# Diagonal blocks packed by ScalarE for one transpose, and a new order of token rows and attention steps, in a fused DeltaNet and sliding-window layer

## The chip, the cores and the metric

The kernel runs on one core of one Trainium2 chip. The metric is the device time of one execution in microseconds (us), inputs in HBM and output back to HBM. Every number is float32.

## What is computed

One layer over 2048 tokens of width 1024. All eight input blocks of a token go through one RMS norm and one projection, whose columns feed two groups of heads:

```python
h = _rmsnorm(x, norm1_w)
gq, gk, gv, gz, gb, ga, aq, ak, av = split(h @ w_in)
# group A: 4 heads, gated delta rule in chunks
lower = strict(kb @ k.T * decay) + I
u, w = inverse(lower) @ (v * beta), inverse(lower) @ (kb * exp(gc))
v_new = u - w @ state
o = q_dec @ state + qk @ v_new
state = state * g_last + k_dec.T @ v_new          # one chunk after another
o_gdn = rms(o) * gdn_norm_w * silu(z)
# group B: 8 heads, window of 128 keys, softmax with a sink
o_attn = softmax(q @ k.T * d**-0.5 - slope * dist, sink) @ v
x = x + concat(o_gdn, o_attn) @ w_out
x = x + relu(rms(x) @ w1)**2 @ w2
```

The kernel takes chunks of 128 tokens ("tiles") for the delta rule, so a triangular 128x128 matrix is inverted for each of 4 heads and 4 tiles of a group.

## The kernel before

The sequence is cut into four groups of 512 tokens, and one loop over `g` runs all stages for a group. Each engine has its own program, written out by hand in order; engines meet only at semaphores, and an instruction that waits holds up all that stand behind it on its engine. Weights come in 96 units a group (a 1024x128 slab, 512 KB). A unit is loaded by SP, split by ScalarE into a high part (`split_hi`, w_h, L400) and by VectorE into a low part (`split_lo`, w_l, L720), and multiplied by TensorE in 24 matmuls (`unit`, all recorded at L1229, like most matmuls). `w_h` and `w_l` have two buffers each.

A group's stages, by their TensorE work:

1. Twelve convolution units, then units for the decay rows, attention v, k and four attention q units. In the loop over `j` of the q units each step also handles tile `t = j` of the delta rule: `decay`, `diagonal`, `products` (VectorE; `products` writes the strictly decayed Gram matrix `at_[:, t]`, signal `at_r`, L876), and `delta` (ScalarE, L506).
2. Four gate units `U_Z + m` (m = 0 to 3; called Z0 to Z3 below). In between come `token_rows(t)`: TensorE transposes v and k of a tile (L1336, L1341) into two PSUM banks, and VectorE scales them out (`value_rows`, signal `vb_r`, L1045; `key_rows`, signals `kb_r` and `kd_r`, L1054, L1056). A bank is used again only when the rows before are out.
3. The triangular inverse. VectorE inverts the 16x16 diagonal blocks: `gather` transposes them out of `at_` into block rows, `block_inverse` runs 19 small steps, `scatter` puts the result into the factors `ti` and `xi`. From there TensorE doubles the blocks over three levels (`masked`, `update`, `turn`).
4. Sixteen attention pairs n are spread over 19 steps `attend(k)` (k = 0 to 18) among levels, key states and tiles: step k starts pair k (`sc` on TensorE, then `scores` on VectorE and `exps` on ScalarE), finishes the softmax sum of pair k-1 on VectorE, whose division GpSimd does (L352), and transposes pair k-2 (`pt`) and multiplies pair k-3 with the values (`ov`) on TensorE.
5. The loop over the four tiles: `values`, `v_copy`, the sum for the next state, `new_state` (VectorE, L1088), the output matmuls, `out_square`, `out_mean`, `out_root` (ScalarE, L616, L618), `gated` (VectorE, L1100, L1105), `mix_hi`, `mix_lo`. `values(t)` waits for the state of tile t-1.
6. Eight output units (starting with `out_part` on the attention half), then the MLP in 64 units.

The orders of stages 2 and 5 in the kernel before, for TensorE:

```python
for m in range(GATE):
    unit(g, CONV, U_Z + m - CONV, A0 + (U_Z + m) % 2, hid)
    if 0 < m < GATE - 1:
        token_rows(m - 1)
...
for t in range(TILES):
    values(t)
    if t: out_mean(t - 1)
    attend(10 + 2 * t)
    if t == TILES - 1: attend(17)
    state_and_out(t)
    attend(11 + 2 * t if t < TILES - 1 else 18)
```

On VectorE, `gather`, `block_inverse` and `scatter` stand after `split_lo` of Z2 and before `split_lo` of Z3; the `vb_r` of tile 0 comes right after. GpSimd clears `ti` and `xi`, does the divisions of pairs 0 to 13, waits for `mlo` of tile 1, issues the load of `xs` and then does pairs 14 and 15.

Of the kernel before, what the change touches and what calls it, by code (L numbers as in the profile page):

```python
# [91 lines left out]
def build(nc, x, w, par, con, bias, out):  # L92
    with ExitStack() as ctx:
# [112 lines left out]
        MAX, NMAX, SUM, SEXP, RDEN = (slice(2 * i, 2 * i + 2) for i in range(5))  # L206

        def first_half(m, l):

            return m.rearrange("p (n two b) -> p n two b", two=2, b=BLOCK << l)[:, :, 0, :]  # L210
# [13 lines left out]
        def mix(t):  # L224

            return kb23[:, t] if t < 2 else qk[:, t - 2]

        def blocks(m, b):
# [4 lines left out]
        def flat(m):  # L233
            return m.rearrange("p h c -> p (h c)")

# [18 lines left out]
        tb_zeroed = ctx.enter_context(nc.semaphore("tb_zeroed"))  # L254
        blk_in = signal("blk_in", QUADS)
        blk_ext = signal("blk_ext", 4)
        blk_out = signal("blk_out", 2 * QUADS)
        blk = signal("blk", 19)
# [76 lines left out]
        def _(pool):  # L335
# [10 lines left out]
            with pool.Fori(0, GROUPS) as g:  # L346
# [16 lines left out]
                pool.nop(nofuse=True)  # L363
                nc.gpsimd.memset(ti[:], 0.0).then_inc(zeroed.sem, 1)
                nc.gpsimd.memset(xi[:], 0.0).then_inc(zeroed.sem, 1)  # L365
                for n in range(14):
                    probabilities(n)
# [3 lines left out]
                pool.dma_start(xs[:], x[g]).then_inc(x_loaded.sem, 16)  # L371
                for n in range(14, TILES * PAIRS):
                    probabilities(n)


# [16 lines left out]
        def _(act):  # L392
# [45 lines left out]
            with act.Fori(0, GROUPS) as g:  # L438
# [75 lines left out]


                act.wait_ge(unit_done.sem, unit_done.after(g, U_BA + 1))
                act.activation(rw[0:32, 0], ps[0:32, A0, :], ACT.Identity, scale=-1.0).then_inc(row_act.sem, 1)
# [24 lines left out]
                for j in range(PAIRS):  # L542
                    t = j
                    act.wait_ge(unit_done.sem, unit_done.after(g, U_AQ + j + 1))
                    act.copy(aq[:, j], ps[:, A0 + (U_AQ + j) % 2, :]).then_inc(copied.sem, 1)
                    split_hi(g, CONV, U_AQ + 2 + j - CONV)
                    norm_root(j)
                    decay(t)
                    key_log(t)
                    query_square(t)  # L550
                    delta(t)
                norm_root(PAIRS)

                act.wait_ge(B1["tok"].sem, B1["tok"].after(g, 1))
# [88 lines left out]
                attend(8)  # L643
                for t in range(TILES):
                    wt(B["p_wt"], t)
                    act.copy(ti[:, t], heads(lev(t))).then_inc(B["wtc"].sem, 1)
                attend(9)
                for t in range(TILES):
                    v_copy(t)
                    if t:  # L650
                        out_root(t - 1)
                    attend(10 + 2 * t)
                    if t == TILES - 1:
                        attend(17)
                    if t:
                        mix_hi(t - 1)
                    out_square(t)
                    attend(11 + 2 * t if t < TILES - 1 else 18)
                out_root(TILES - 1)
# [51 lines left out]
        def _(dve):  # L711
# [61 lines left out]
            with dve.Fori(0, GROUPS) as g:  # L773
# [131 lines left out]
                dve.tensor_scalar(sm[:, :, CB], sm[:, :, EGC], -1.0, None, ALU.mult).then_inc(B1["c1"].sem, 1)  # L905
                split_lo(g, CONV, U_Z + 2 - CONV)

# [10 lines left out]

                def quad(m, r):

                    return m[r][:, :, :, r].rearrange("j t h (b i) -> j i b (t h)", b=2)

                def by_block(m):

                    return m.rearrange("p (i b x) -> p i b x", b=2, x=BLOCK)
# [13 lines left out]

                def scatter():  # L940

                    flip = d1[:, 0].rearrange("p h c -> p (h c)")
                    rows = tb[:, 0:BLOCK * BLOCK].rearrange("p (r c) -> p r c", c=BLOCK)
                    for b in range(2):
                        own_half = prm[:, C_BLK + b:C_BLK + b + 1]
                        dve.tensor_scalar(by_block(tmp[:])[:, :, b], rows.rearrange("p r c -> p c r"), own_half, None,
                                          ALU.mult).then_inc(blk_ext.sem, 1)
                        dve.tensor_scalar(by_block(flip)[:, :, b], rows, own_half, None, ALU.mult).then_inc(blk_ext.sem, 1)
                    own(blk_ext, g, 4)
                    dve.wait_ge(zeroed.sem, zeroed.after(g, 2))  # L950
                    for n in range(QUADS):
                        r = slice(32 * n, 32 * n + 32)
                        dve.transpose(quad(ti, r), by_block(tmp[r])).then_inc(blk_out.sem, 1)
                        dve.transpose(quad(xi, r), by_block(flip[r])).then_inc(blk_out.sem, 1)

                def block_inverse():
# [183 lines left out]
                attend(8)  # L1140
                attend(9)
                for t in range(TILES):
                    attend(10 + 2 * t)
                    if t == TILES - 1:
                        attend(17)
                    if t:
                        gated(t - 1)
                    new_state(t)
                    attend(11 + 2 * t if t < TILES - 1 else 18)
                    out_square(t)  # L1150
                    if t:
                        mix_lo(t - 1)
# [74 lines left out]
        def _(pe):  # L1227
# [29 lines left out]
            with pe.Fori(0, GROUPS) as g:  # L1257
# [198 lines left out]

                def state_and_out(t):

                    wt(B["vnc"], t)
                    four(heads(outb(t, 1)), lambda o, h: mm(o, part(1, t)[:, h], v_new(t)[:, h]), B["p_su"])  # L1460
                    wt(B["qd_r"], t)
# [41 lines left out]
                attend(8)  # L1503
                for t in range(TILES):
                    key_states(t)
                attend(9)
                for t in range(TILES):
                    values(t)
                    if t:
                        out_mean(t - 1)  # L1510
                    attend(10 + 2 * t)
                    if t == TILES - 1:
                        attend(17)
                    state_and_out(t)
                    attend(11 + 2 * t if t < TILES - 1 else 18)

# [193 lines left out]
```

## Time and profile before

| | |
|---|---|
| median of 3 runs | 2623.86 us (2623.4 to 2624.37) |
| profiled execution | 2619.94 us, of it a span of 2618.4 us from first to last instruction |
| mean granted TensorE clock | 0.984 |
| busy: PE, DVE, ACT, POOL | 95%, 56%, 37%, 5% |
| HBM traffic | 88 GB/s over the span |

In the rows below PE is the matmul side of TensorE, DVE is VectorE, ACT is ScalarE and POOL is GpSimd. A row of a timeline has its start in us from the start of the span, its duration in us, the engine, the line, the operation, what it writes and reads, and how many instructions it merges; in brackets stands how long the engine was idle before it and what ended that. All four groups look alike; where no group is named, the rows are those of the first, whose stages 2 to 5 lie between 157 and 285 us.

### The profile page before, as it was taken

To read this page: it belongs to the slowest core of one execution; us is meant where nothing else is said; L and a number is where in the kernel's file an instruction comes from. 1 tells how busy PE (TensorE), PEld (TensorE's weight loads), DVE (VectorE), ACT (ScalarE), POOL (GpSimd) and SP (SyncE) were. 2 spreads that over 40 slices of the span, in tenths; PEclk is the share of its full clock that TensorE was granted. 3 is DMA by queue.
4 is the path that set the end of the run, shared out by engine and by line. 5 is a ranking of instruction groups with operands and counts; after the bars stand their busy time and mean duration, and the time that the engine had idled before them with its cause. 6 is when DMAs were issued, how large, how long until landed. Compare 5 with 4: busy or idle time off the path is not lost.

```text
span 2618.4 us, 36125 instructions
## 1 busy us (share of the span) xinstructions
PE 2490.5 (95%) x12446; PEld 2046.3 (78%) x12446; DVE 1463.5 (56%) x2220; ACT 957.8 (37%) x1741; POOL 129.6 (5%) x149
## 2 busy tenths in 40 slices
PE   5979999999997999999999799999999979999998
PEld 4868788888876778888887677888888767788887
DVE  5676564364667646345466765634556675552554
ACT  4436432223353733222335363222234536321222
POOL 0012000000000200000000120000000011000000
PEclk9989999999998999999999899999999989999999
DMA  4210223224321022233332112232432211232242
GB/s 148 96 49 18 89 89 102 92 96 152 106 88 41 25 90 97 96 96 120 129 106 81 41 42 81 96 99 94 138 116 101 73 33 47 91 98 97 94 140 77
DMA packets 62019, 233.16 MB, mean 89 GB/s; under 512 B 7232, under 2 KB 7232, under 8 KB 61248
## 3 DMA queue, kind: packets, MB, share of 16 engines
q1 hardware_dynamic: 55728, 202.64, 23.5%
q0 software_dynamic: 6160, 28.84, 3.0%
q8 instruction: 74, 1.21, 0.2%
q14 instruction: 57, 0.47, 0.1%
HBM read 223.06 MB, written 8.39 MB: 88 GB/s over the span
## 4 chain that ended last, share of the span: by engine, by line
PE 80%; issue 11%; DVE 4%; ACT 2%; POOL 2%; DMA 0%; ACTq 0%; POOLq 0%; DVEq 0%; SPq 0%
PE ps L1229 79%; POOL pp L352 1%; PE ps L1376 1%; ACT w_h L400 1%; DVE acc L728 0%; DVE w_l L720 0%; DMA stage<-w 0%; POOL xi L365 0%; DVE row L839 0%; DVE h_l L1168 0%; DVE cy L786 0%; DVE ht L734 0%; DVE nq L798 0%; DVE h_l L1110 0%; DVE h_l L1030 0%
## 5 line engine op out<-in xcount | busy, mean ns | idle before, releaser
L1229 PE MATMUL ps<-h_h,w_h 128*128 128x512 f32 x2016 | 800.9, 397 | 25.1 <-DVE h_l L1168 8.9
L1229 PE MATMUL ps<-h_l,w_h 128*128 128x512 f32 x2016 | 789.6, 392 | 0.0
L1229 PE MATMUL ps<-h_h,w_l 128*128 128x512 f32 x2016 | 789.3, 391 | 0.0
L720 DVE TENSOR_TENSOR w_l<-stage,w_h 128x1024 fp32r<-128x1024 f32 (+1 forms) x385 | 467.9, 1215 | 315.1 <-ACT w_h L400 302.7
L400 ACT CAST w_h<-stage 128x1024 fp32r<-128x1024 f32 (+1 forms) x385 | 399.9, 1039 | 579.6 <-PE ps L1229 571.3
L1229 PEld LDWEIGHTS ps<-h_h,w_h 128*128 128x128 f32 x2016 | 381.6, 189 | 119.5 <-issue 23.1
L1229 PEld LDWEIGHTS ps<-h_h,w_l 128*128 128x128 f32 x2016 | 381.5, 189 | 80.6
L1229 PEld LDWEIGHTS ps<-h_l,w_h 128*128 128x128 f32 x2016 | 382.0, 190 | 79.6 <-issue 2.9
L1229 PE MATMUL ps<-ff_h,w_h 128*128 128x512 f32 x1024 | 400.0, 391 | 0.0
L1229 PE MATMUL ps<-ff_h,w_l 128*128 128x512 f32 x1024 | 398.4, 389 | 0.0
L1229 PE MATMUL ps<-ff_l,w_h 128*128 128x512 f32 x1024 | 398.4, 389 | 0.0
L684 ACT ACTIVATE ff_h<-fb 128x512 f32 (+1 forms) x128 | 81.1, 633 | 482.3 <-DVE fb L1182 482.3
L1229 PEld LDWEIGHTS ps<-ff_h,w_h 128*128 128x128 f32 x1024 | 192.2, 188 | 40.9 <-issue 1.0
L1229 PEld LDWEIGHTS ps<-ff_l,w_h 128*128 128x128 f32 x1024 | 192.2, 188 | 40.7 <-issue 1.0
L1229 PEld LDWEIGHTS ps<-ff_h,w_l 128*128 128x128 f32 x1024 | 192.2, 188 | 39.8
L1182 DVE SCALAR_TENSOR_TENSOR fb<-ps,rt 128x512 f32<-128x512 f32 x128 | 88.6, 692 | 232.4 <-PE ps L1229 220.7
L1201 DVE TENSOR_TENSOR xs<-ps,xs 128x512 f32 (+1 forms) x64 | 44.3, 693 | 187.8 <-PE ps L1229 187.8
L786 DVE SCALAR_TENSOR_TENSOR cy<-raw,prm,cy 128x512 f32<-128x512 f32 x144 | 108.0, 750 | 14.6 <-DVE cy L782 6.9
L1189 DVE TENSOR_TENSOR ff_l<-ff,ff_h 128x512 f32 (+1 forms) x128 | 88.7, 693 | 27.8 <-ACT ff_h L684 15.5
L1186 DVE TENSOR_TENSOR ff<-fb 128x512 f32<-128x512 f32 x128 | 88.6, 692 | 13.3 <-DVE fb L1182 8.5
L450 ACT COPY raw<-ps 128x512 f32<-128x512 f32 x48 | 28.2, 587 | 148.6 <-PE ps L1229 148.6
L352 POOL TENSOR_TENSOR pp<-pp,att 128x384 f32<-128x384 f32 x64 | 63.3, 992 | 333.5 <-DVE att L1024 333.5
(195 smaller groups left out, 2045.6 us busy)
## 6 DMA issues: line engine op xcount, KB each, us to landing
stage<-w SPq DMA_DIRECT2D x385, 512.0 KB, 3.3
x_next<-x POOLq DMA_DIRECT2D x20, 512.0 KB, 6.3
xs<-x POOLq DMA_DIRECT2D x4, 2048.0 KB, 8.0
out<-xs POOLq DMA_DIRECT2D x32, 256.0 KB, 2.3
bia<-bias POOLq DMA_DIRECT2D x1, 1536.0 KB, 7.1
cst<-con SPq DMA_DIRECT2D x1, 704.0 KB, 4.9
prm<-par SPq DMA_DIRECT2D x1, 39.5 KB, 1.8
```

The source lines that it names most:

```text
L352: nc.gpsimd.tensor_tensor(pp[:, n % 2, :, HD:], pp[:, n % 2, :, HD:], att[:, n % 2, RDEN].unsqueeze(2).to_broadcast([P, 2, KEYS]), ALU.mul ...
L400: act.copy(w_h[:, b, 0:k], stage[:, s, 0:k]).then_inc(w_hi.sem, 1)
L450: act.copy(raw[:, s % 2, 3:], ps[:, A0 + s % 2, :]).then_inc(raw_ready.sem, 1)
L684: act.activation(ff_h[:, i * 4 + s, :], fb[:, s % 2], ACT.Square).then_inc(fh_ready.sem, 1)
L720: dve.tensor_tensor(w_l[:, b, 0:k], stage[:, s, 0:k], w_h[:, b, 0:k].bitcast(F32), ALU.subtract).then_inc(w_lo.sem, 1)
L786: dve.scalar_tensor_tensor(out=cy[:, s % 2], in0=raw[:, s % 2, j:j + TOK], scalar=convw(prm, m, j), in1=cy[:, s % 2], op0=ALU.mult, op1=AL ...
L1182: dve.scalar_tensor_tensor(out=fb[:, s % 2], in0=ps[:, s % 2, :], scalar=0.0, in1=rt[:], op0=ALU.max, op1=ALU.mult).then_inc(fb_ready.sem, 1)
L1186: dve.tensor_tensor(ff[:, s % 2], fb[:, s % 2], fb[:, s % 2], ALU.mult).then_inc(fp_ready.sem, 1)
L1189: dve.tensor_tensor(ff_l[:, i * 4 + s, :], ff[:, s % 2], ff_h[:, i * 4 + s, :].bitcast(F32), ALU.subtract).then_inc(ff_ready.sem, 1)
L1201: dve.tensor_tensor(xs[:, m, :], ps[:, s // 2 % 2, :], xs[:, m, :], ALU.add).then_inc(res.sem, 1)
L1229: return pe.matmul(o, a, b, start=start, stop=stop)
L1376: last = pe.transpose(o[:, e, c], pp[:, n % 2, e, c * P:c * P + P], I)
```

## The change

It has three parts.

The first is the way of the diagonal blocks. Before, `gather` made four transposes of 32 partitions straight out of `at_`. Now ScalarE copies the blocks of each tile as soon as `at_` is written (`pack`, four copies of 32 partitions a tile, 16 in a group) side by side into the first quarter of `xi`, and `gather` is one transpose over 128 partitions. `xi` is cleared by GpSimd only after that. `scatter` keeps its eight transposes; its four scaling instructions are ordered by target, with a wait after the first two.

The second is the order around it. On VectorE `split_lo` of Z2 moves behind `gather`, and `split_lo` of Z3 from behind `scatter` to the middle of `block_inverse`. On TensorE the token rows of tiles 0 and 1 come one gate unit later: behind Z2 and Z3.

The third is the order of the last attention steps: each goes one place sooner from `attend(10)` on, and `state_and_out` is split, so that in the last tile `attend(18)` stands before the output matmuls. On ScalarE `out_root` and `mix_hi` of the tile before now stand behind the attention step. GpSimd issues the load of `xs` after all 16 pairs.

```diff
+        def quadrant(n):
+            return slice(32 * n, 32 * n + 32)
+        diag_in = flat(xi[:, 0])
...
         @block.gpsimd
                 nc.gpsimd.memset(ti[:], 0.0).then_inc(zeroed.sem, 1)
+                pool.wait_ge(blk_in.sem, blk_in.after(g, 1))
+                pool.nop(nofuse=True)
                 nc.gpsimd.memset(xi[:], 0.0).then_inc(zeroed.sem, 1)
-                for n in range(14):
+                for n in range(TILES * PAIRS):
                     probabilities(n)
 
                 pool.wait_ge(B["mlo"].sem, B["mlo"].after(g, 2))
                 pool.nop(nofuse=True)
                 pool.dma_start(xs[:], x[g]).then_inc(x_loaded.sem, 16)
-                for n in range(14, TILES * PAIRS):
-                    probabilities(n)
...
         @block.scalar
+                def pack(t):
+                    wt(B["at_r"], t)
+                    act.nop(nofuse=True)
+                    for n in range(QUADS):
+                        r = quadrant(n)
+                        act.copy(by_block(diag_in[r])[:, :, :, HEADS * t:HEADS * t + HEADS].rearrange("j i b h -> j h b i"),
+                                 at_[r, t][:, :, r].rearrange("j h (b i) -> j h b i", b=2)).then_inc(packed.sem, 1)
...
                     query_square(t)
                     delta(t)
+                    if t < TILES - 1:
+                        pack(t)
                 norm_root(PAIRS)
+                pack(TILES - 1)
...
+                w_copy(0)
+                w_copy(1)
                 attend(9)
+                w_copy(2)
+                w_copy(3)
+                attend(10)
                 for t in range(TILES):
                     v_copy(t)
+                    attend(11 + 2 * t)
                     if t:
                         out_root(t - 1)
-                    attend(10 + 2 * t)
+                        mix_hi(t - 1)
                     if t == TILES - 1:
-                        attend(17)
-                    if t:
-                        mix_hi(t - 1)
+                        attend(18)
                     out_square(t)
-                    attend(11 + 2 * t if t < TILES - 1 else 18)
+                    if t < TILES - 1:
+                        attend(12 + 2 * t)
...
         @block.vector
-                split_lo(g, CONV, U_Z + 2 - CONV)
...
                 def gather():
-                    own(B["at_r"], g, TILES)
-                    for n in range(QUADS):
-                        r = slice(32 * n, 32 * n + 32)
-                        dve.transpose(by_block(tmp[r]), quad(at_, r)).then_inc(blk_in.sem, 1)
-                    own(blk_in, g, QUADS)
+                    dve.wait_ge(packed.sem, packed.after(g, packed.per_group))
+                    dve.transpose(tmp[:], diag_in).then_inc(blk_in.sem, 1)
+                    own(blk_in, g, 1)
...
                     for b in (4, 8):
+                        if b == 8:
+                            split_lo(g, CONV, U_Z + 3 - CONV)
...
                 gather()
+                split_lo(g, CONV, U_Z + 2 - CONV)
                 block_inverse()
                 scatter()
-                split_lo(g, CONV, U_Z + 3 - CONV)
...
                 attend(8)
                 attend(9)
-                for t in range(TILES):
-                    attend(10 + 2 * t)
-                    if t == TILES - 1:
-                        attend(17)
+                attend(10)
+                for t in range(TILES):
+                    attend(11 + 2 * t)
                     if t:
                         gated(t - 1)
                     new_state(t)
-                    attend(11 + 2 * t if t < TILES - 1 else 18)
+                    attend(12 + 2 * t)
                     out_square(t)
...
         @block.tensor
                     unit(g, CONV, U_Z + m - CONV, A0 + (U_Z + m) % 2, hid)
-                    if 0 < m < GATE - 1:
-                        token_rows(m - 1)
+                    if m >= 2:
+                        token_rows(m - 2)
...
-                for t in range(TILES):
-                    key_states(t)
+                key_states(0)
+                key_states(1)
                 attend(9)
+                key_states(2)
+                key_states(3)
+                attend(10)
                 for t in range(TILES):
                     values(t)
                     if t:
                         out_mean(t - 1)
-                    attend(10 + 2 * t)
+                    attend(11 + 2 * t)
+                    state_sum(t)
                     if t == TILES - 1:
-                        attend(17)
-                    state_and_out(t)
-                    attend(11 + 2 * t if t < TILES - 1 else 18)
+                        attend(18)
+                    tile_out(t)
+                    if t < TILES - 1:
+                        attend(12 + 2 * t)
```

## Rows read from the trace of the kernel before

**Rows 1.** The page's chain that ended last, shares by engine.
```profile
PE 80%; issue 11%; DVE 4%; ACT 2%; POOL 2%; DMA 0%; ACTq 0%; POOLq 0%; DVEq 0%; SPq 0%
```

**Rows 2.** Waits, whole span: who waited for whom, us, times, longest.
```profile
PE ps L1336 <- DVE qkvz L1045: 56.9, 4, 14.2
```

**Rows 3.** Timeline of PE, first group, gate units to first level.
```profile
168.29 0.60 PE L1336 MATMUL ps<-cst,qkvz 128*128 128x128 f32 x4
...
188.99 1.11 PE L1336 MATMUL ps<-cst,qkvz 128*128 128x128 f32 x4 [14.18 <-DVE qkvz L1045]
...
198.41 1.90 PE L1229 MATMUL ps<-ti,at 128*128 128x64 f32 x16
```

**Rows 4.** Timeline of DVE, first group, products of tile 2 to key rows.
```profile
150.85 0.69 DVE L876 SCALAR_TENSOR_TENSOR at<-ps,dt 128x512 f32<-128x512 f32 x1 [1.28 <-ACT dt L506]
...
165.31 4.46 DVE L932 STREAM_TRANSPOSE tmp<-at 32x512 f32<-32x512 f32 x4
...
171.02 0.17 DVE L958 COPY tb<-gb 128x8 f32<-128x8 f32 x1
...
174.34 1.05 DVE L984 TENSOR_TENSOR tmp<-gb,tb 128x512 f32<-128x512 f32 x1
...
188.25 0.69 DVE L1045 TENSOR_TENSOR qkvz<-ps,sm 128x512 f32<-128x512 f32 x1
...
191.95 0.68 DVE L1056 TENSOR_TENSOR qkvz<-ps,sm 128x512 f32<-128x512 f32 x1
```

**Rows 5.** Timeline of ACT, first group: a query copy and Z2's split.
```profile
152.78 0.59 ACT L545 COPY aq<-ps 128x512 f32<-128x512 f32 x1 [1.97 <-PE ps L1229]
...
163.08 1.05 ACT L400 CAST w_h<-stage 128x1024 fp32r<-128x1024 f32 x1
```

**Rows 6.** A group of ACT instructions by shape: count, busy us, mean ns.
```profile
L536 ACT COPY vt<-vt 128x128 f32<-128x128 f32 x1 | 0.3, 302 | 0.0
```

**Rows 7.** Windows: length, busy of engines, granted clock, DMA share, GB/s.
```profile
179.00:180.00 1.00, 0.00 (x0) 0.00 (x0) 0.87 (x3) 0.00 (x0) 0.00 (x0) 0.65 0.00 0
...
192.00:193.00 1.00, 1.00 (x4) 0.81 (x3) 0.63 (x2) 0.00 (x0) 0.00 (x0) 0.52 0.92 344
```

**Rows 8.** Timeline of PE, first group, the loop over the tiles.
```profile
257.29 0.39 PE L1229 MATMUL ps<-qkvz,xi 128*128 128x128 f32 x2
...
259.08 1.02 PE L1229 MATMUL ps<-at,cst 128*128 128x512 f32 x2
...
267.82 1.02 PE L1229 MATMUL ps<-at,cst 128*128 128x512 f32 x2
...
270.62 0.66 PE L1376 MATMUL ps<-cst,pp 128*128 128x128 f32 x4 [1.19 <-POOL pp L352]
```

**Rows 9.** Timeline of DVE, first group, the same loop.
```profile
260.67 0.56 DVE L1010 SCALAR_TENSOR_TENSOR ss<-ps,bia 128x384 f32<-128x384 f32 x1 [0.91 <-PE ps L1229]
...
261.85 0.16 DVE L1015 SCALAR_TENSOR_TENSOR att<-att,nsink 128x2 f32<-128x2 f32 x1
...
262.79 0.74 DVE L1100 SCALAR_TENSOR_TENSOR kb<-ps,prm,kb 128x512 f32<-128x512 f32 x1
...
264.17 1.12 DVE L1088 SCALAR_TENSOR_TENSOR state<-state,sm,ps 128x128 f32<-128x128 f32 x4
```

**Rows 10.** Timeline of ACT, first group, the same loop.
```profile
260.14 0.69 ACT L616 ACTIVATE kb<-ps,eps 128x512 f32<-128x512 f32 x1 [0.28 <-PE ps L1229]
260.86 0.63 ACT L618 ACTIVATE kb<-kb 128x512 f32<-128x512 f32 x1
...
262.34 0.47 ACT L576 ACTIVATE pp<-ss,att 128x192 f32<-128x192 f32 x1
...
263.23 0.47 ACT L580 ACTIVATE att<-att,prm 128x1 f32<-128x1 f32 x2
```

**Rows 11.** Windows of groups 1 and 4, pair 8 to the last output half.
```profile
233.20:284.81 51.61, 47.54 (x386) 38.59 (x385) 30.63 (x78) 33.49 (x95) 10.41 (x11) 1.00 0.15 52
...
2164.70:2217.50 52.80, 49.20 (x389) 40.12 (x386) 30.37 (x78) 33.65 (x95) 10.52 (x11) 0.97 0.14 51
```

More of the change, by code:

```diff
@@ L206, in build, with flat @@
         MAX, NMAX, SUM, SEXP, RDEN = (slice(2 * i, 2 * i + 2) for i in range(5))
+        def flat(m):
+            return m.rearrange("p h c -> p (h c)")
         def first_half(m, l):
@@ L226, in mix, with by_block, quad @@
             return kb23[:, t] if t < 2 else qk[:, t - 2]
+        def by_block(m):
+            return m.rearrange("p (i b x) -> p i b x", b=2, x=BLOCK)
+        def quadrant(n):
+            return slice(32 * n, 32 * n + 32)
+        def quad(m, r):
+            return m[r][:, :, :, r].rearrange("j t h (b i) -> j i b (t h)", b=2)
+        diag_in = flat(xi[:, 0])
+        diag_ti, diag_xi = flat(dt_[:, 0]), flat(dt_[:, 1])
         def blocks(m, b):
@@ L231, in blocks @@
                 "p m (r c) -> p m r c", c=BLOCK)
-        def flat(m):
-            return m.rearrange("p h c -> p (h c)")
         def per_head(m):
@@ L254, in build @@
         tb_zeroed = ctx.enter_context(nc.semaphore("tb_zeroed"))
-        blk_in = signal("blk_in", QUADS)
+        blk_in = signal("blk_in", 1)
         blk_ext = signal("blk_ext", 4)
+        packed = signal("packed", QUADS * TILES)
         blk_out = signal("blk_out", 2 * QUADS)
@@ L643, in _, with w_copy @@
                 attend(8)
-                for t in range(TILES):
+                def w_copy(t):
                     wt(B["p_wt"], t)
                     act.copy(ti[:, t], heads(lev(t))).then_inc(B["wtc"].sem, 1)
+                w_copy(0)
+                w_copy(1)
                 attend(9)
+                w_copy(2)
+                w_copy(3)
+                attend(10)
                 for t in range(TILES):
                     v_copy(t)
+                    attend(11 + 2 * t)
                     if t:
                         out_root(t - 1)
-                    attend(10 + 2 * t)
+                        mix_hi(t - 1)
                     if t == TILES - 1:
-                        attend(17)
-                    if t:
-                        mix_hi(t - 1)
+                        attend(18)
                     out_square(t)
-                    attend(11 + 2 * t if t < TILES - 1 else 18)
+                    if t < TILES - 1:
+                        attend(12 + 2 * t)
                 out_root(TILES - 1)
@@ L917, in over_last @@
                     return m.unsqueeze(len(m.shape)).to_broadcast(list(m.shape) + [n])
[L919 to L925, printed above, removed]
                 def gather():
-                    own(B["at_r"], g, TILES)
-                    for n in range(QUADS):
-                        r = slice(32 * n, 32 * n + 32)
-                        dve.transpose(by_block(tmp[r]), quad(at_, r)).then_inc(blk_in.sem, 1)
-                    own(blk_in, g, QUADS)
+                    dve.wait_ge(packed.sem, packed.after(g, packed.per_group))
+                    dve.transpose(tmp[:], diag_in).then_inc(blk_in.sem, 1)
+                    own(blk_in, g, 1)
                     to = gb[:, 0:BLOCK * BLOCK].rearrange("p (j i) -> p j i", i=BLOCK)
@@ L940, in scatter, with halves @@
                 def scatter():
-                    flip = d1[:, 0].rearrange("p h c -> p (h c)")
+                    turned = flat(d1[:, 0])
                     rows = tb[:, 0:BLOCK * BLOCK].rearrange("p (r c) -> p r c", c=BLOCK)
[L944 to L949, printed above, removed]
+                    def halves(to, m, n):
+                        for b in range(2):
+                            dve.tensor_scalar(by_block(to)[:, :, b], m, prm[:, C_BLK + b:C_BLK + b + 1], None,
+                                              ALU.mult).then_inc(blk_ext.sem, 1)
+                        own(blk_ext, g, n)
+                    halves(tmp[:], rows.rearrange("p r c -> p c r"), 2)
+                    halves(turned, rows, 4)
                     dve.wait_ge(zeroed.sem, zeroed.after(g, 2))
                     for n in range(QUADS):
-                        r = slice(32 * n, 32 * n + 32)
+                        r = quadrant(n)
                         dve.transpose(quad(ti, r), by_block(tmp[r])).then_inc(blk_out.sem, 1)
-                        dve.transpose(quad(xi, r), by_block(flip[r])).then_inc(blk_out.sem, 1)
+                        dve.transpose(quad(xi, r), by_block(turned[r])).then_inc(blk_out.sem, 1)
                 def block_inverse():
@@ L1455, in values, with state_sum, tile_out @@
                     last.then_inc(B["p_vv"].sem, 1)
-                def state_and_out(t):
+                def state_sum(t):
                     wt(B["vnc"], t)
                     four(heads(outb(t, 1)), lambda o, h: mm(o, part(1, t)[:, h], v_new(t)[:, h]), B["p_su"])
+                def tile_out(t):
                     wt(B["qd_r"], t)
```

## The prediction

> **What bounds the kernel now.** I read the chain of waits first: TensorE sets 80% of it and time in which nothing is shown to be waited for another 11% [rows 1]. So only two things move the end: TensorE's idle time, and the work of other engines that it waits for. I then went through TensorE's own waits, longest first. In the first group the longest by far is the 14.18 us ahead of the token rows of tile 1, ended by VectorE's value rows [rows 3]; the same wait stands once in each of the four groups, 56.9 us in all [rows 2]. The reader is to see what VectorE does in it: from 165.31 to 188.25 it gathers, inverts, scatters and splits Z3, and only then writes the rows out that free the bank [rows 4]. In that time TensorE has no split of Z3 to work with, and its clock falls to half about 4.5 us after its last matmul and comes back 4 us after work starts again [rows 3, 7]. The second place is the loop over the tiles: the stretch from pair 8 to the attention half of the output takes 51.61 us with 47.54 busy, so 4.1 us of waiting [rows 11], 1.19 of them for GpSimd, which issues the load of xs between two divisions [rows 8].
>
> **First part: gather and its order.** After the change ScalarE packs tile 3 before the three small exponentials, the table load and the split of Z2. A copy of 128x128 takes 0.30 us [rows 6], and I take 0.25 us for each following one here, so 1.0 us for four. Below, 0.2 (such instructions overlap a little). Above, 0.5: the copy writes single elements 128 bytes apart, and the nearest row of a strided pattern is VectorE's 1.05 us for 512 elements, against 0.69 us of a plain one [rows 4], so the element part may well grow. The Trainium skill speaks against this edit: "SBUF — State Buffer", under "Door 1: The DMA port swizzle", says that an access pays a penalty each time it leaves a 16-byte line, which these writes do at every element. No row here shows it for ScalarE; by that page I would go to the upper value.
>
> So the high half of Z2, which ended at 164.13 [rows 5], ends at about 165.2. VectorE meanwhile does the one transpose and the two selects. The transpose costs between 0.69 us (a plain 512-element instruction) and 1.1 us (a quarter of the 4.46 us for four) [rows 4]; I take 1.0, from 162.8 to 163.8, then 1.2 for the selects, to 165.0. Either way VectorE next waits for ScalarE, and the price of the transpose does not count. Split of Z2: 165.2 to 166.4; TensorE needs it at 168.3, so it stays hidden. The inverse begins at 166.4 in place of 171.02: **4.6 us sooner**. From the inverse to the value rows VectorE's work is what it was, 171.02 to 188.25 (the split of Z3 only sits elsewhere inside, and the clearing of xi ends near 166, long before scatter), so vb_r of tile 0 comes at 184.3 in place of 188.9.
>
> TensorE: the split of Z3 is there at 166.4 + 3.3 (171.02 to 174.34) + 1.2 = 170.9. Z2 and then the token rows of tile 0 take the 6.5 us that they took in the other order (168.29 to 174.8), and Z3, 24 matmuls, 5.5 us more; TensorE is idle from about 180.3 to 184.4. Then it is paced by VectorE: value and key rows of tiles 0 and 1, six instructions of 0.6 us pitch, one small split, end at 192.63 before [rows 4], which is 4.4 us after 188.25, at half clock and with a wait for a transpose. At full clock I get 3.3 us, so 187.6, the key transposes of tile 2 end 0.45 us later, and the first level starts at 188.0 in place of 198.41 [rows 3]: **10.4 us sooner**. Against it stands the clock. About 4 us of idleness and then 4 us of half-busy transposes is what let it fall before [rows 7], so in some groups it falls; then the transposes cost 0.5 to 1 us more and the first level starts at half rate, up to 2 us. I take 1.5 us: **-8.9 us a group**, bounds -10.4 and -7.4.
>
> The pack of tiles 0 to 2 sits at the end of a step of ScalarE. at_ is written at 151.54 and the next query copy starts at 152.78 [rows 4, 5]: 1.2 us of cover, which 1.0 us just fits. At 2.0 us ScalarE would slip 0.8 us a step, and TensorE some 2 us over the steps.
>
> **Second part: the attention order.** TensorE's work is the same, so only waits count. Before, a tile takes 8.74 us (259.08 to 267.82) with no wait [rows 8]. Now the root of tile t-1 stands on ScalarE behind the exponentials of a pair, and VectorE's gating of t-1 stands ahead of new_state(t), for which values(t+1) waits. From the start of out_mean(t-1): 1.6 to the start of scores (259.08 to 260.67), 1.34 scores, 1.36 exponentials, 1.35 root, 1.38 gating, 1.12 state [rows 8 to 10], and 0.3 of handing over: 8.4 us. TensorE has meanwhile 0.93 of out_mean, 1.6 of an attention step, 0.9 for the state sum, 1.9 for the outputs and 1.6 of a step (estimates from the same stretch): 6.9 for t = 1, and 6.4 for t = 2, whose second step starts no pair. So values(2) waits 1.4 us and values(3) 2.0 us. Before, the root stood ahead of the step, and this chain was 2.7 us shorter. Next late is out_mean(1): its sum stands on VectorE behind new_state, the scores and a cast (1.3 + 0.3 + 0.6 + 0.6 = 2.8) while values takes 1.8 (257.29 to 259.08): 1.1 us more. Tile 3 has root, gating and mix_hi of tile 2 ahead of the last attention copy, so the output half waits 1.9 us. With 0.6 us at pair 6, as before, that is 7.0 us against 4.1, although GpSimd's wait is gone: **+2.9 us a group**. The load of xs, issued some 4 us later, still lands before its use. More gaps mean more fallen clocks: group 4 has one in this stretch and takes 1.2 us more than group 1 [rows 11]. Two groups had such a fall; I take it in all, +0.6 us. Sum of the part **+3.5 us**, bounds +1.5 and +5.
>
> **Sum.** (-8.9 + 3.5) x 4 = -21.6 us. The profiled execution took 2619.94 us, so 2598.3 in its terms; it lies 3.9 us under the median 2623.86, so the median should become **2602.3 us**. The likeliest case's own range: -10.4 + 1.5 gives -36 and -7.4 + 5 gives -10, so 2588 to 2614.
>
> **Rivals.** (a) The attention order costs nothing and gives what it looks like: both chains fit under TensorE's work, which they do if they are 2 us shorter than I add up. Then only about 1 us of the 4.1 stays: (-8.9 - 3.1) x 4 = -48, 2576 us. For it: pair 14 and 15 no longer wait for GpSimd. Against it: the rows add up. (b) The pack is slow (0.5 us a copy): 1.0 us more ahead of the inverse and about 1.6 us in the steps, 2.6 us a group less gain, 10 us over four: 2613 us. Against it: ScalarE writes 128 elements a copy, so even a doubled element part adds little to the 0.30 us row. By the 16-byte rule named above this is the likelier case. (c) The new waits feed each other (scores late, so exponentials late, so roots late) and cost 8 us in place of 2.9: the net is about -1 us a group, 2620 us, no difference. (d) On the other side: in the loop over the tiles the gaps let the clock fall and keep it low. That stretch has 47.5 us of TensorE work [rows 11]; each fall costs about 2 us until the clock is back. It decides from three falls a group on (5.4 us); with five it is +10 - 5.4 = +4.6 a group, 2642 us. Gaps of 1 to 2 us between 7 us of dense work hardly do that: before, at most one fall a group is seen.
>
> **Chances.** My forecast 0.70, (a) 0.12, (b) 0.08, (c) 0.06, (d) 0.04. A difference under 0.2% (5 us) cannot be told from none. Faster 0.90 (forecast, (a), (b)), same 0.06, slower 0.04. The range leaves out (a), (c) and (d): 2585 to 2614.
>
> **What would show it.** Right: in the gate stage Z2 and Z3 back to back with one wait of about 4 us behind Z3, ended by the value rows; the first level near 188 in the first group; the one transpose under 1.2 us; four pack copies in about 1 us; in the loop over the tiles waits of TensorE for VectorE's state of 1.4 and 2 us, and a stretch from pair 8 to the output half near 54.5 us. Wrong: a first level later than 191; the query units waiting for a split; or no wait at all in the tile loop, which would put the result at (a).

## The result: 0.4% slower

The changed kernel takes 2631.22 us, median of 10 executions (2622.54 to 2639.79), against 2620.85 us of the kernel before, also of 10 (2618.44 to 2624.37). The ratio is 1.004 (95% interval 1.0026 to 1.0054). I had forecast 22 us less. The profiled execution is the fastest of the ten, with a span of 2621.0 us, so its trace shows less of the loss than the median has. Over the ten the time follows the mean granted clock: 0.985 in the fastest, 0.981 near the median, 0.978 in the slowest. Two things in the figures were not in my sum: the median is slower, and the times spread over 17 us where those of before spread over 6.

The page's chain by engine:
```profile
PE 76%; issue 11%; DVE 5%; ACT 5%; POOL 1%; DMA 0%; ACTq 0%; DVEq 0%; POOLq 0%; SPq 0%
```
Against [rows 1], ScalarE and VectorE have taken 4 points from TensorE: more of the work of others is now on the path.

The timeline of TensorE in the first group, gate units to the first level (start, duration, instruction, idle before):
```profile
173.98 0.60 PE L1363 MATMUL ps<-cst,qkvz 128*128 128x128 f32 x4
...
186.72 1.11 PE L1363 MATMUL ps<-cst,qkvz 128*128 128x128 f32 x4 [6.22 <-DVE qkvz L1073]
...
191.32 2.03 PE L1256 MATMUL ps<-ti,at 128*128 128x64 f32 x16
```
This is the shape that I had forecast: the 14.2 us wait of [rows 3] is 6.2 us now, and the first level starts at 191.3, not 198.4. It is not the size: I had 188.0, and this group had been 1.7 us ahead when its query units began. Counted from the first query copy, the first level starts 69.9 us later in place of 75.4, so some 5.4 us sooner and not 10.4. VectorE in the same stretch:
```profile
163.23 0.93 DVE L939 TENSOR_SCALAR sm<-sm 128x16 f32<-128x16 f32 x1 [1.03 <-ACT sm L583]
163.34 0.82 DVE L955 STREAM_TRANSPOSE tmp<-xi 128x512 f32<-128x512 f32 x1
164.22 2.04 DVE L959 TENSOR_SCALAR gb<-tmp,prm 128x256 f32<-128x256 f32 x1
166.30 0.69 DVE L960 SCALAR_TENSOR_TENSOR gb<-tmp,prm,gb 128x256 f32<-128x256 f32 x1
167.12 1.23 DVE L754 TENSOR_TENSOR w_l<-stage,w_h 128x1024 fp32r<-128x1024 f32 x1
168.26 0.17 DVE L984 COPY tb<-gb 128x8 f32<-128x8 f32 x1
...
185.98 0.69 DVE L1073 TENSOR_TENSOR qkvz<-ps,sm 128x512 f32<-128x512 f32 x1
```
and GpSimd's two clearings:
```profile
162.32 1.81 POOL L380 MEMSET ti<- 128x2048 f32 x1 [2.03 <-DVE aq L840]
164.31 1.81 POOL L383 MEMSET xi<- 128x2048 f32 x1 [0.17 <-DVE tmp L955]
```
The one transpose is cheap, 0.82 us against 4.46. But the two scalings next to it take 0.93 and 2.04 us, and both end just as a clearing ends (164.16 and 164.13; 166.26 and 166.12). The pack on ScalarE, tile 2:
```profile
150.80 1.69 ACT L537 COPY xi<-at 32x128 f32<-32x128 f32 x4 [0.81 <-DVE at L910]
152.51 0.59 ACT L570 COPY aq<-ps 128x512 f32<-128x512 f32 x1
```
Its four copies take 1.7 us, and the query copy has no idle time ahead of it any more: ScalarE has become the pace of the query units.

The stage of the levels, from the first level to the key states, took 37.0 us in all four groups of before, at full clock. Groups 1 and 2 of before:
```profile
198.40:235.40 37.00, 35.80 (x347) 30.94 (x346) 27.34 (x71) 22.04 (x70) 7.66 (x7) 1.00 0.05 17
842.90:879.90 37.00, 35.79 (x347) 30.94 (x346) 27.34 (x71) 22.01 (x70) 7.66 (x7) 1.00 0.06 17
```
In the changed kernel, windows of groups 1 to 4 (length, busy of PE, PEld, DVE, ACT and POOL, granted clock, DMA share, GB/s):
```profile
191.30:228.40 37.10, 35.90 (x346) 31.04 (x345) 26.96 (x70) 20.91 (x69) 7.67 (x7) 1.00 0.05 16
831.50:871.00 39.50, 38.29 (x346) 33.44 (x346) 27.25 (x70) 20.91 (x69) 7.67 (x7) 0.93 0.05 16
1476.90:1523.50 46.60, 45.73 (x346) 40.28 (x345) 27.28 (x70) 21.11 (x69) 7.66 (x7) 0.76 0.04 13
2127.80:2164.70 36.90, 35.70 (x346) 30.85 (x345) 26.95 (x70) 20.91 (x69) 7.67 (x7) 1.00 0.05 17
```
The same 346 matmuls, and up to 9.6 us longer at a granted clock of 0.76: the half clock (1.2 GHz of the full 2.4) now lies over the levels. Before, it had ended inside Z3, as two windows of the first group of before show:
```profile
192.50:193.00 0.50, 0.50 (x3) 0.40 (x2) 0.13 (x1) 0.00 (x0) 0.00 (x0) 0.54 1.02 401
193.00:193.50 0.50, 0.50 (x4) 0.41 (x3) 0.00 (x0) 0.00 (x0) 0.00 (x0) 1.00 0.43 172
```
TensorE's waits from the key states to the output in the first group (who waited for whom, us, times, longest):
```profile
PE ps L1256 <- DVE state L1116: 3.3, 2, 1.9
PE ps L1256 <- DVE h_l L1058: 1.9, 1, 1.9
PE ps L1256 <- DVE at L1123: 0.9, 1, 0.9
PE ps L1403 <- POOL pp L368: 0.5, 1, 0.5
```
Those are the four waits that I had added up for the tile loop (3.4, 1.9, 1.1 and 0.6 us).

Read off both traces, the stages of a group add up as follows (sums over the four groups, us):

| from | to | before | changed |
|---|---|---|---|
| first query copy | fourth query copy | 118.9 | 124.6 |
| fourth query copy | start of the inverse | 73.0 | 63.0 |
| start of the inverse | first value rows | 69.0 | 70.8 |
| first value rows | first level | 42.2 | 21.0 |
| first level | key states | 147.9 | 160.2 |
| key states | first output add | 212.4 | 229.1 |

So up to the key states 11.4 us are gained, and the last row loses 16.7. The stages outside the table differ by under 3 us.

### The profile page after: what moved, and what is told of

Read it like the earlier page. It is cut to its first block, busy times and chain, and to the rows that moved or that the text cites. A ratio compares the mean times of both kernels' runs of the same rounds, so it can differ in the third digit from the quotient of the medians.

```text
span 2621.0 us, 36201 instructions
## 1 busy us (share of the span) xinstructions
PE 2507.5 (96%) x12446; PEld 2058.1 (79%) x12446; DVE 1459.2 (56%) x2208; ACT 984.2 (38%) x1805; POOL 130.0 (5%) x149
## 4 chain that ended last, share of the span: by engine, by line
PE 76%; issue 11%; DVE 5%; ACT 5%; POOL 1%; DMA 0%; ACTq 0%; DVEq 0%; POOLq 0%; SPq 0%
PE ps L1256 75%; POOL pp L368 1%; ACT w_h L415 1%; PE ps L1403 1%; ACT xi L537 1%; ACT dt L521 1%; DVE nq L832 0%; DVE state L1116 0%; DVE acc L762 0%; DVE w_l L754 0%; DVE sm L896 0%; ACT pp L604 0%; DMA stage<-w 0%; DVE at L894 0%; DVE d L888 0%
## 5 line engine op out<-in xcount | busy, mean ns | idle before, releaser
L604 ACT ACTIVATE pp<-ss,att 128x192 f32<-128x192 f32 x128 | 57.4, 453 | 84.5 <-DVE att L1043 84.5
```

Source lines behind the costliest of these rows:

```text
L604: act.activation(pp[:, b, e, HD:], ss[:, b, e], ACT.Exp, bias=att[:, b, NMAX][:, e:e + 1], accum_out=att[:, b, SUM][:, e:e + 1])
```

## The experiments

All times are medians, and each ratio is to the kernel before run on the same chip, whose median lies between 2619.95 and 2622.01 us. The changed kernel was not run again beside them, so a difference to its 2631.22 us crosses chips and can be off by some 2 us.

**undo_attention.** All four engines get back the attention and tile-loop order of before; the rest of the change stays.

```diff
-                    attend(11 + 2 * t)
-                    state_sum(t)
-                    ...
+                    attend(10 + 2 * t)
+                    if t == TILES - 1:
+                        attend(17)
+                    state_and_out(t)
+                    attend(11 + 2 * t if t < TILES - 1 else 18)
```

> The changed kernel with the attention and tile-loop order of before on all four engines; packing and token rows as changed. Theory A (the new attention order costs 3.5 us a group by the chain root, gating, state): 14 us less than the changed kernel, about 2617 us. Theory B (the order is harmless and the half clock behind the late token rows takes everything): as the changed kernel, about 2631 us, with the stretch from the key states to the output still 56 us.

Measured 2600.16 us, ratio to before 0.9935 (0.9913 to 0.9957). So packing and token rows together are a gain of 20 us, and the attention order on top of them costs 31. Theory A has the sign, but its 14 us is half of that. In the two traces the stretch from the key states to the output add accounts for 15.0 of the 31 us (229.1 against 214.1), and the levels for 9.8: undo_attention also has half clock there, but no group like the third of the changed kernel. Its groups 2 and 3:
```profile
829.20:868.70 39.50, 38.30 (x347) 33.45 (x346) 27.25 (x70) 20.89 (x69) 7.66 (x7) 0.93 0.05 16
1470.30:1507.30 37.00, 35.80 (x347) 30.95 (x346) 27.06 (x71) 20.89 (x69) 7.66 (x7) 1.00 0.05 17
```

**only_attention.** The kernel before with only the third part of the change, the reverse of the edit above.

> The kernel before with only the new attention and tile-loop order. Theory A: 3.5 us a group more than before, so about 2635 us, and waits of TensorE for VectorE's state of 1.5 to 2 us in tiles 2 and 3. Theory B: no slower than before, 2621 us or a little less.

Measured 2636.01 us, ratio 1.0063 (1.0046 to 1.0079): 16 us more, as theory A has it. The waits are those of the changed kernel:
```profile
PE ps L1231 <- DVE state L1091: 3.4, 2, 1.9
PE ps L1231 <- DVE h_l L1033: 1.9, 1, 1.9
PE ps L1231 <- DVE at L1098: 0.9, 1, 0.9
```

**filler_after.** Useless transposes ("filler") in the hole behind Z3.

```diff
+                    if m == GATE - 1:
+                        for _ in range(48):
+                            pe.transpose(ps[:, PT, 0:P], I, I)
                     if m >= 2:
                         token_rows(m - 2)
```

> The changed kernel with 48 useless 128x128 transposes (5.3 us) behind Z3, in the 6 us in which TensorE waits for the value rows. Theory C (half clock during the rows and the levels costs 16 us in the profiled execution and about 25 in the median one): no half clock there, about 2606 us, and executions that agree within a few us. Rival: the clock is not what spreads the times, and nothing changes: 2631 us, spread as before.

Measured 2612.61 us, ratio 0.9979 (0.9966 to 0.9992): 19 us less than the changed kernel for work that does nothing. The clock is a cost of its own, three quarters of the 25 us expected. In two groups of the trace some half clock was still left in the rows or the levels (5.1 us in the levels of group 3). The spread (2610 to 2622 us) is smaller, not gone.

**memset_late.** Both clearings behind the selects and the first copy.

```diff
+                pool.wait_ge(blk_in.sem, blk_in.after(g, 1))
+                pool.wait_ge(blk.sem, blk.after(g, 3))
+                pool.nop(nofuse=True)
                 nc.gpsimd.memset(ti[:], 0.0).then_inc(zeroed.sem, 1)
-                pool.wait_ge(blk_in.sem, blk_in.after(g, 1))
-                pool.nop(nofuse=True)
                 nc.gpsimd.memset(xi[:], 0.0).then_inc(zeroed.sem, 1)
```

> The changed kernel with both of GpSimd's clearings behind the selects of gather and the first copy of the inverse. Theory D (VectorE's two scaling instructions, 0.93 and 2.04 us in place of 0.16 and 0.46, are held up by the clearings that run beside them): these two are back at 0.16 and 0.46 us, the inverse starts 2.2 us sooner, 9 us less in all, 2622 us if the clock does not take it. Rival: the strided source of the select is slow after a 128-partition transpose: still 2.04 us, 2631 us.

Measured 2618.51 us, ratio 1.0002 (0.9986 to 1.0018), 13 us less than the changed kernel. VectorE's timeline:
```profile
163.09 0.17 DVE L940 TENSOR_SCALAR sm<-sm 128x16 f32<-128x16 f32 x1 [1.02 <-ACT sm L584]
163.20 0.71 DVE L956 STREAM_TRANSPOSE tmp<-xi 128x512 f32<-128x512 f32 x1
163.95 0.47 DVE L960 TENSOR_SCALAR gb<-tmp,prm 128x256 f32<-128x256 f32 x1
164.45 0.70 DVE L961 SCALAR_TENSOR_TENSOR gb<-tmp,prm,gb 128x256 f32<-128x256 f32 x1
165.67 1.23 DVE L755 TENSOR_TENSOR w_l<-stage,w_h 128x1024 fp32r<-128x1024 f32 x1 [0.53 <-ACT w_h L416]
```
The scalings are back at 0.17 and 0.47 us, and VectorE now waits 0.53 us for Z2's high half: the order of waits that my prediction had drawn. Theory D holds in its cause, not in its size: because of that wait for ScalarE the inverse starts 1.3 us sooner than in the changed kernel (14.4 us after the fourth query copy in place of 15.8), not the 2.2 us expected. That is 5 us in four groups. The rest of the 13 us has no place in the traces; the executions spread from 2612 to 2630 us. The clearings run here beside tensor-tensor and reduce instructions and hold up none of them.

**root_first.** One move on ScalarE.

```diff
                     v_copy(t)
-                    attend(11 + 2 * t)
                     if t:
                         out_root(t - 1)
+                    attend(11 + 2 * t)
+                    if t:
                         mix_hi(t - 1)
```

> The changed kernel with one instruction pair moved: on ScalarE out_root(t-1) stands ahead of the attention step again, everything else of the new order stays. If the root behind the exponentials is what lengthens the chain to the next state, the waits for the state go and the stretch from the key states to the output falls from 56.1 to about 50.5 us (52.5 before): some 20 us less than the changed kernel, 2609 us. Rival (it is the attention step sooner itself, or the split state sum): still 56 us, 2631 us.

Measured 2601.16 us, ratio 0.9927 (0.9907 to 0.9947): 30 us less than the changed kernel by that move. The waits for the state are gone:
```profile
PE ps L1404 <- POOL pp L368: 0.5, 1, 0.5
PE ps L1257 <- DVE h_l L1059: 0.2, 1, 0.2
PE ps L1257 <- DVE h_l L1139: 0.2, 1, 0.2
PE ps L1257 <- DVE at L1124: 0.2, 1, 0.2
```
From the key states to the first output add it takes 49.9 us in the first group, against 56.1 in the changed kernel and 52.5 before. Over the four groups it is 199.6 us against 229.1, so this stretch alone gives the 30 us: some 25 of waits, and some 5 because three groups of the changed kernel had 3.4 us of half clock there and root_first has none. I had expected 20 us, without the clock. Half clock in the levels stays: one group of root_first takes 46.5 us there.

**pack_only.** The kernel before with `pack`, the one transpose and the later clearing of xi; splits, token rows and attention as they were.

> The kernel before with only the packing, the one transpose and the later clearing of xi; splits, token rows and attention as before. Theory E (the packing costs 1.4 us in the query units, delays Z2's split by 1.7 us and lets the clearing hold a select, 1.5 us, for 3.6 us saved): no gain, 2622 to 2630 us. Rival (the shorter gather pays): 2610 us or less.

Measured 2625.51 us, ratio 1.0015 (1.0006 to 1.0024). The packing alone loses 3.5 us. Its first select (the scaling of 256 elements behind the transpose) shows the 2.04 us again, beside the clearing.

**no_pack_undo.** The other way round: undo_attention with the four transposes out of `at_` and no pack.

> undo_attention (2600 us) without the packing: the four transposes out of at_ as before, both clearings early as before, the splits and token rows in the new order. Theory E (packing costs as much as it gives: 1.4 us a group in the query units, 0.9 in front of Z2's split and 2.3 by the clearing, against 3.6 us for the transposes): within 5 us of 2600. Rival (the packing is where the gain comes from): 12 us or more above it.

Measured 2601.73 us, ratio 0.9922 (0.99 to 0.9943), the same as undo_attention within the spread. So the whole gain of 20 us comes from the order of splits and token rows; the packing, as made, gives nothing. The traces say what it trades: a group takes 46.3 us from the first query copy to the inverse without the packing, 46.9 with it, and 45.5 with it and the late clearings (memset_late). So it would pay a little once the clearings are out of its way; no run tests that alone.

**filler_before.** 120 transposes in the 14 us hole of the kernel before.

> The kernel before with 120 useless transposes (13 us) in the 14 us in which TensorE waits for the value rows. There the half clock is over before the levels begin, and only Z3's first matmuls and two row transposes run in it: about 1.5 us a group less, 6 us, 2615 us. If the half clock were a cost of before as large as of the changed kernel, 2600 us or less.

Measured 2620.19 us, ratio 0.9992 (0.9982 to 1.0001). I had expected 6 us less; it is 1.8, and the interval reaches from 0.3 us more to 4.7 less. The half clock was in the hole of before too (granted clock 0.54 from 820 to 832 us, against 1.00 here), and cost little there: when TensorE came back it had one unit to do before the levels. The test is not quite clean: two groups of this trace still have 3.4 us of half clock ahead of the levels, and VectorE reaches the value rows 0.4 us later in each group.

**undo_filler_memset and root_filler_memset.** The late clearings and 40 transposes behind Z3, with the old attention order and with the new one and the root ahead.

> undo_attention with the late clearings and 40 useless transposes behind Z3. Clearings: 1.5 to 2 us a group. Clock: full during rows and levels in most groups, another 1.5 us a group. About 2587 us. Rival (the two do not add, since a sooner start only meets the half clock elsewhere): 2595 to 2600 us.

> The changed kernel with all three repairs: root ahead of the step, late clearings, 40 useless transposes behind Z3. The stretch from key states to output at 50.5 us against 52.5 in undo_filler_memset: 8 us less than that, about 2580 us. Rival: the new attention order never pays, 2587 us or more.

Measured 2582.41 us (ratio 0.9863, 0.9833 to 0.9893) and 2582.53 us (0.9867, 0.9838 to 0.9897). Late clearings and filler together take 18 us off undo_attention and 19 off root_first. That is well past the rival's 2595 us, but less than the 13 and 19 us that they took singly off the changed kernel, so they do not simply add. The first ranges from 2581 to 2596 us and the second from 2575 to 2596, in four executions each, so these two do not say what the attention order is worth.

**all_repairs.** root_filler_memset with 46 transposes, and five more in the rows.

```diff
                     four(heads(VROW), lambda o, h: pe.transpose(o, part(2, t)[:, h], I), B["p_vt"])
+                    if t in (1, 2):
+                        for _ in range(5):
+                            pe.transpose(ps[:, PT, 0:P], I, I)
```

> root_filler_memset with 46 transposes behind Z3 and five more between the value and key rows of tiles 1 and 2, so that TensorE is also busy while VectorE writes rows. If what still spreads root_filler_memset (2575 to 2596 us) is half clock that begins in these rows: all executions near 2575 us. If it begins elsewhere (tile loop, later stages): as before, 2582 us.

Measured 2575.69 us (2572.72 to 2576.16, five executions), ratio 0.982 (0.9807 to 0.9834). The spread has gone, and the time is 46 us under the kernel before. This is the fastest version. As the edit adds six transposes behind Z3 too, it does not say which of the two places took the spread away. Windows of groups 1 and 2 from pair 8 to the last output half (the stretch of [rows 11]):
```profile
225.80:274.70 48.90, 47.84 (x385) 38.77 (x384) 30.94 (x78) 33.58 (x94) 10.05 (x11) 1.00 0.16 55
859.00:908.00 49.00, 47.94 (x387) 38.80 (x385) 31.04 (x78) 33.68 (x95) 10.14 (x11) 1.00 0.15 55
```

**repairs_new_root and repairs_old_attention.** all_repairs with the root behind the step again, and with the attention order of before.

> all_repairs (2575.7 us) with out_root(t-1) behind the attention step, as in the changed kernel. With the clock kept up, only the chain is left: the stretch from key states to output was 56.1 us against 49.9, so 6.2 us a group, 25 us: 2600 us. If the wrong place of the root also lets the clock fall in the tile loop: 2605 to 2615 us and half clock there in the trace.

> all_repairs with the attention and tile-loop order of before. That stretch at 52.5 us against 49.9: 2.6 us a group, 10 us more, 2586 us; that would be what the new attention order is worth with the root in its old place. Rival: the same 2575.7 us.

Measured 2604.87 us (ratio 0.993, 0.9913 to 0.9947) and 2581.44 us (0.9852, 0.9836 to 0.9869). The root's place is worth 29 us, the rest of the attention order a gain of 6, where 10 were expected (the runs are on different chips; taken against their own runs of the kernel before, the two are 31 and 8). In the traces the stretch from the key states to the output add takes 52.1 us a group in the old order and 49.9 in all_repairs. The first has half clock again, and up to the output only in the tile loop; its windows of groups 1 and 2, same stretch:
```profile
223.80:280.50 56.70, 49.92 (x386) 39.84 (x384) 30.72 (x78) 32.82 (x95) 10.45 (x11) 0.97 0.14 48
864.00:920.70 56.70, 50.09 (x381) 39.86 (x380) 29.76 (x77) 32.29 (x94) 10.52 (x11) 0.94 0.13 47
```
Granted clocks of 0.97 and 0.94 over 56.7 us are 3.4 and 6.8 us at half clock; all_repairs has none there. TensorE's longest wait in that stretch is 1.9 us. So gaps of 1 to 2 us in the tile loop did let the clock fall, once or twice a group.

## Why the prediction was wrong, step by step

- **TensorE's hole and the order around it.** Right in kind. Z2 and Z3 run back to back, the wait behind them is ended by the value rows, and this order is the gain: 20 us in no_pack_undo.
- **The step that failed.** It is the first part, "-8.9 us a group" with bounds of -10.4 and -7.4. That makes 36 us; the trace has 11.4 up to the key states, while the second part, 14 us forecast, is 16.7 there. Three terms of the first part were mis-sized, and the next three points take them in turn: the clock behind the hole (6 us forecast, 15.4 in the trace, more in the median), the start of the inverse (18.4 us sooner forecast, 10.0 measured) and the pack in the query units (nothing forecast, 5.7 measured). None of the three alone turns the sign.
- **What the clock costs behind the hole.** I took 1.5 us a group, with 3 us as the worst, because I let the half clock reach only the first level. In the profiled execution it took 2.5 and 9.6 us of the level stage in two groups and nothing there in the others, on top of 0.5 to 0.9 us a group in the rows (5.3 us, in one group 4.9, against 4.5 in all_repairs). filler_after got 19 us back in the median, 4.7 us a group. What I missed is what stands behind the hole. Before, a dense gate unit came first, and the clock was back within it; the change moves that unit ahead of the hole, and what is left behind it is rows and levels. There the half clock lasted up to 22 us of a stage (group 3). The other traces agree: in before, only_attention, pack_only and filler_before, all with Z3 behind the hole, the levels take 37.0 us in every group, while the changed kernel, undo_attention, root_first, memset_late and no_pack_undo each have groups of 39.4 to 46.6 us. Why it lasts next to nothing in one group and 22 us in another stays open.
- **The pack in the query units.** I had it fit its 1.2 us of cover at 0.25 us a copy. It takes 0.43: the three steps from the first query copy to the fourth take 31.1 us in place of 29.7. That is my rival (b), at four fifths of its price: 1.4 us a group there and 0.7 ahead of the inverse, 2.1 of the 2.6 us. The trace has 417 ns a copy of 128 elements in 32 partitions, written 128 bytes apart, against 302 ns of the plain one [rows 6]. By the 16-byte rule of the Trainium skill's "SBUF — State Buffer", "Door 1: The DMA port swizzle", such writes pay at each element; the trace agrees in direction, but no run changes the stride alone.
- **"Either way VectorE next waits for ScalarE."** False. The scalings beside the clearings took 2.3 us more, and the split of Z2 came after them. The inverse starts 15.8 us after the fourth query copy against 18.2 before, 2.5 us sooner and not 4.6. Of the 2.1 us missing, the clearings make 1.3, as memset_late shows by giving them back, and the slower pack the rest. The Trainium skill has this rule, in "SBUF — State Buffer" under "Who interferes with whom": scaling and copy instructions of VectorE can take the pair of ports that it shares with GpSimd, and then one waits for the whole instruction of the other. The trace agrees (both scalings end within 0.15 us behind a clearing's end), and I had not looked for it, as the clearings used to run beside a split and transposes only.
- **The sum of the first part against undo_attention.** Predicted -36 us in all. Taking off 1.4 (query units), 2.1 (inverse) and 0.5 us a group (the inverse to the value rows takes 17.7 in place of 17.2) leaves -20, and undo_attention measured -20. There the clock's share happens to be about what I had put in: 5 us in its trace, against 6. That is luck, as the changed kernel shows with 15.4 us by the same order around the hole.
- **The attention order.** Mechanism and size right as far as the waits go. Alone it costs 16 us against +14 predicted (only_attention). In the first group the stretch from the key states to the output add takes 56.1 us against 52.5, and from pair 8 to the output half the changed kernel takes 55.2 against the 54.5 that I had named. Rival (a) would have needed the chain without the misplaced root: with the root ahead of the step, root_first takes 49.9 us.
- **Rival (d)**, gaps in the tile loop that let the clock fall, got 0.04 and the remark that such gaps hardly do that. In the changed kernel's trace they do it once in three groups, where before had it in two. With the repairs it is once or twice a group: repairs_new_root is 23.4 us over repairs_old_attention, where the waits alone make 3.9 x 4 = 15.6, which leaves about 8 us for the clock. Two falls a group are fewer than the three that I had named as deciding, and it did not make the sign. The sign came from the whole: a gain of 20, a loss of 31.
- **What stays open.** On top of the first two parts the attention order costs 31 us, on the kernel before only 16. In the two profiled executions 15 of the 31 are waits in the tile loop and 10 are half clock in one group's levels. The rest lies between the profiled execution and the median. The mean granted clocks, 0.981 near the median of the changed kernel and 0.988 in undo_attention, make some 38 us more at half clock, which by my estimate is worth up to 19 us (half of it); so waits and clock together can hold the 31. What is not shown is why the half clock lasts longer with the new attention order. The two orders start the later groups at other moments, and with few executions of undo_attention (2598 to 2611 us in five) part of it can be chance.

## What to carry to other kernels

A hole in TensorE's work is priced by its length and by what comes right behind it. Here a dense unit behind the hole had the clock back before it ended, while short dependent steps ran at half clock for up to 22 of a stage's 46.6 us. Filling the hole with useless matmuls paid 19 us; leaving a dense unit behind it may do as well, but no run tests that by itself. When an instruction is moved behind another on an in-order engine, add up the loop in which it stands, across all engines, and compare it with the work that covers it; each wait summed in this way was right here to 0.2 us. Put no term at nothing because it "just fits" its cover: the pack had 0.2 us to spare at the guessed price and overran it at the real one. And when a clearing or another GpSimd instruction moves, look at which VectorE instructions it now runs beside.

## What the runs showed of the hardware

- GpSimd's clearing of 128x2048 (1.81 us) held VectorE's scaling of SBUF data until its end: 2.04 us in place of 0.46 for 256 elements, 0.93 in place of 0.16 for 16, in all four groups. Tensor-tensor and reduce instructions beside it kept their durations (memset_late), and four block transposes beside both clearings took 4.52 us (no_pack_undo) against 4.46.
- VectorE's 32x32 block transpose of 128 partitions with 512 contiguous elements took 0.71 us (memset_late); of 32 partitions with a strided side, 1.0 to 1.1 us.
- With TensorE busy on filler transposes, VectorE's scatter transposes took 1.07 to 1.08 and 1.03 to 1.06 us in place of 1.03 to 1.04 and 0.99 to 1.01 (first group), and filler_before lost 0.4 us a group on the way to the value rows.
